# Last block of a hybrid decoder step: projection tiles, gating groups and norm steps in another order

## The reference, cut to what matters

```python
h = rms_norm(x, g_norm) * (1 + scale) + shift
p = h @ w_in                      # h_A, B_A, C_A, z_A, u_B, v_B, z_B
# group A: short gated convolution
s = c_a * h_a
conv = conv_w[0]*s_pad[:, 0:t] + conv_w[1]*s_pad[:, 1:t+1] + conv_w[2]*s_pad[:, 2:t+2]
y_a = b_a * conv * silu(z_a)
# group B: spatial gating in chunks of 128 positions
v_n = layer_norm(v_b, g_v, b_v)
y_b = u_b * (tril(W_s) v_n + b_s) * silu(z_b)
y = concat([y_a, y_b]) @ w_out
out = rms_norm(x + gate * y, g_final)
```

## Time and profile before

| | us |
|---|---|
| median of 3 runs | 347.27 (346.55 to 347.93) |
| the profiled execution | 346.61 |
| its span, slowest core (core 2) | 344.8 |
| spans of all 8 cores | 341.0 to 344.8 |
| TensorE busy, core 2 | 292.3 (85%) |
| VectorE busy, core 2 | 187.4 (54%) |
| GpSimd busy, core 2 | 110.6 (32%) |

### The profile page before, as it was taken

How to read it: one execution, slowest core, us unless ns; L and a number is a source line. 1 busy time by engine, 2 the same in 40 slices (tenths; PEclk the granted TensorE clock), 3 DMA queues, 4 the chain that set the end, 5 groups by cost and what they waited for, 6 DMA issues and landing times.

```text
span 344.8 us, 5627 instructions; the slowest of 8 cores (341.0 to 344.8 us)
## 1 busy us (share of the span) xinstructions
PE 292.3 (85%) x1792; PEld 152.1 (44%) x1792; DVE 187.4 (54%) x350; ACT 122.1 (35%) x215; POOL 110.6 (32%) x161
## 2 busy tenths in 40 slices
PE   0328269996999996999999999999999999999940
PEld 0223134443444443444455444445555557776410
DVE  0321025356464641755778846557864567658972
ACT  2511024127353205624436343444615234242320
POOL 7390265123424213412225443112322122222210
PEclk9999859999999998999999999999999999999995
DMA  5999999999999982075113515101260101516223
GB/s 158 213 156 173 162 165 173 164 230 227 176 176 159 151 183 78 29 204 192 64 60 124 197 49 147 61 22 74 90 237 10 32 0 63 183 63 197 86 117 123
DMA packets 14157, 44.51 MB, mean 129 GB/s; under 512 B 1968, under 2 KB 2352, under 8 KB 13104
## 3 DMA queue, kind: packets, MB, share of 16 engines
q0 software_dynamic: 6624, 21.24, 34.9%
q1 hardware_dynamic: 7504, 22.91, 20.4%
HBM read 51.02 MB, written 8.85 MB: 174 GB/s over the span
## 4 chain that ended last, share of the span: by engine, by line
PE 53%; DMA 24%; DVE 8%; issue 5%; POOL 3%; another core or an unknown queue 3%; ACT 1%; DVEq 1%; POOLq 0%; SPq 0%; ACTq 0%
PE pb L477 32%; PE pb L704 12%; DMA win_bf<-win_l 12%; DMA wada<-wada_l 11%; PE pb L592 5%; DVE ob L802 2%; DMA xc<-x_p 2%; PE pb L403 1%; PE pb L656 1%; PE pb L814 1%; POOL xa L314 1%; DVE ob L723 1%; DVE ob L720 1%; DVE ob L721 1%
## 5 line engine op out<-in xcount | busy, mean ns | idle before, releaser
L477 PE MATMUL pb<-hT,win_bf 128*128 128x512 bf16 (+3 forms) x680 | 127.6, 344 | 3.6 <-ACT tmp L550 2.0
L477 PEld LDWEIGHTS pb<-hT,win_bf 128*128 128x128 bf16 x680 | 66.4, 98 | 60.0 <-issue 6.3
L704 PE MATMUL pb<-wout_bf,yT 128*128 128x512 bf16 (+1 forms) x256 | 58.2, 379 | 1.3 <-POOL yT L676 1.2
L477 PE MATMUL pb<-hT,wh 128*128 128x512 bf16 (+3 forms) x280 | 54.8, 357 | 2.8 <-DVE hT L423 2.8
L676 POOL TENSOR_TENSOR yT<-tmp,tmp 128x512 bf16<-128x512 f32 (+3 forms) x20 | 22.0, 1100 | 67.2 <-DVE tmp L666 38.6
L551 POOL TENSOR_TENSOR yT<-tmp,tmp 128x512 bf16<-128x512 f32 (+3 forms) x20 | 23.7, 1186 | 59.5 <-DVE tmp L546 40.7
L733 ACT ACTIVATE junk<-ob 128x1024 bf16<-128x1024 f32 (+1 forms) x16 | 16.9, 1057 | 70.7 <-DVE ob L723 57.4
L477 PEld LDWEIGHTS pb<-hT,wh 128*128 128x128 bf16 x280 | 27.8, 100 | 27.8 <-issue 7.7
L532 DVE SCALAR_TENSOR_TENSOR tmp<-spad,pv,tmp 128x512 f32<-128x512 f32 (+2 forms) x40 | 26.7, 667 | 20.4 <-ACT tmp L525 13.1
L704 PEld LDWEIGHTS pb<-wout_bf,yT 128*128 128x128 bf16 (+1 forms) x256 | 23.9, 98 | 28.9 <-issue 1.9
L592 PE MATMUL pb<-wv_bf,hT 128*128 128x512 bf16 (+1 forms) x136 | 30.3, 379 | 0.0
(11 more groups left out here) (88 smaller groups left out, 263.5 us busy)
## 6 DMA issues: line engine op xcount, KB each, us to landing
y_p<-ob SPq DMA_DIRECT2D x15, 512.0 KB, 2.7
xc<-x_p SPq DMA_DIRECT2D x14, 512.0 KB, 6.8
wada<-wada_l POOLq DMA_DIRECT2D x6, 1024.0 KB, 34.1
xa<-x_p POOLq DMA_DIRECT2D x10, 512.0 KB, 36.3
win_bf<-win_l POOLq DMA_DIRECT2D x17, 256.0 KB, 40.5
xa<-x_p SPq DMA_DIRECT2D x8, 512.0 KB, 5.1
wout_bf<-wout_l POOLq DMA_DIRECT2D x2, 1024.0 KB, 55.6
wh<-winh_l POOLq DMA_DIRECT2D x4, 256.0 KB, 25.9
```

Source lines behind the costliest of these rows:

```text
L477: ii = pe.matmul(bk.t[:, 0:B.N], lhsT=wsl(m, k), rhs=hT[B.h][:, k, 0:B.N], start=(k == 0), stop=(k == 7))
L704: ii = pe.matmul(bk.t[R, :], lhsT=yT[B.y][:, k, ti * 128:ti * 128 + P], rhs=wout_bf[:, n, k, :], start=(k == 0), stop=(k == 7))
```

## The change

In the last block's second loop, the C step of a tile of the block ahead (`C_mm`, `C_s1`) is issued in front of `GB(B, j)` instead of behind it. `mid` of `GB(B, j)` is now `C_sq` of tile j, not of tile j - 1. `C_s2` of tile j - 1 comes before `GB(B, j)`, between `C_mm` and `C_s1` of tile j. `C_s3` of tile j - 1 stays at the end of step j, which is now behind `GB(B, j)`. At j = 0 the due `C_s3` of the sample rows goes ahead of `newconv`. The set of instructions and their sizes are the same.

```diff
--- before.py
+++ after.py
@@ -1043,17 +1043,18 @@
             newconv(B)
         for j in range(4):
             if last:
-                GB(B, j, (lambda j=j: C_sq(PV, j - 1)) if 0 < j <= npv else None)
+                if j < npv:
+                    C_mm(PV, j, 0, 8)
                 if j > 0:
                     C_s2(PV, j - 1)
                 if j < npv:
-                    C_mm(PV, j, 0, 8)
                     C_s1(PV, j, False)
+                GB(B, j, (lambda j=j: C_sq(PV, j)) if j < npv else None)
                 if j == 0:
-                    newconv(B)
                     while cq:
                         C_s3(*cq.pop(0))
-                elif j < 4:
+                    newconv(B)
+                else:
                     C_s3(PV, j - 1)
                 continue
             if not late and not last:
```

## The result

The changed kernel takes 351.75 us (median of 4 runs, 350.58 to 352.24). The kernel before takes 347.22 us beside it (median of 4, 346.55 to 347.93). The ratio is 1.012, with a 95% interval of 1.0087 to 1.0153: the change costs 4.5 us, between 3.0 and 5.3. The forecast was 350.4 us with a range up to 351.3. So the sign and the mechanism were right, and the size was too small: the median lies 0.45 us above the range. Some executions of every kernel show a lower granted clock on the cores of one die and take some 6% or more longer; the medians, ratios and cores read here leave them out.

A forecast was written before the change was run, and what follows sets the result against it. VectorE was taken to set the last block's pace, with L720 of tile 0 deciding the end. An order loss of 1.83 us plus 1.14 to 1.67 for half clock led to 347.27 + 3.1 = 350.4 us, range 348.7 to 351.3.

The forecast's parts named there:

- the cost of the order: Last block, core 2: tile 0 ends at 331.53, so L720 starts at 331.71 against 329.88, 1.83 us later at full clock.
- What goes: VectorE before tile 0's L720: the 1.42 us power wait and 1.20 us of L802 leave the path, gaining at most 0.90.
- The first cost: VectorE at the first residual load: group 0 now stands behind L723, so the wait grows from 1.33 to 2.05 us.
- The second cost: Slice 6 comes last: group 2's L666 on VectorE starts at 325.52, its GpSimd product at 326.14.
- The third cost: GpSimd's group 2 product, slowed beside tile 1's L802, ends at 327.76, not 326.87; tile 0 starts on TensorE at 327.90.
- TensorE's side: Group 3's matmuls end at 324.4; TensorE idles 3.5 us until 327.90, then tile 0's 16 matmuls take 3.63 us.
- The clock: After that idle stretch TensorE most likely runs tile 0's 16 matmuls at half clock, costing 1.14 to 1.67 us more.
- (a): Late slice 6, slowed GpSimd and half clock: core 2 loses 3.0 to 3.5 us, kernel 350.1 to 350.8; chance 0.62.
- Case (e): Half clock over both last tiles, or longer load waits: up to 4.5 us, kernel to 351.8; chance 0.10.
- (b): TensorE's clock stays up before tile 0: loss 1.83 us, kernel 349.1; chance 0.15.
- (c): GpSimd isn't slowed, idle stretch 2.6 us: loss 0.94 to 2.6 us, kernel 348.2 to 349.9; chance 0.10.
- (d): TensorE isn't held by slice 6, group 2's L666 before about 323.0: 0.90 us won, kernel 346.4; chance 0.03.

The follow-up runs named there:

- the experiment on it: Changed kernel with tile 1's scaling (L802) moved from behind group 2 to behind group 3: 347.68 us, ratio 1.0084 to the kernel before.
- the second run: The changed kernel, unedited, measured once more on the second chip: 348.94 us, ratio 1.0123 to the kernel before.

## Why the prediction was wrong in size and right in kind

Two steps failed: the cost of the order, put at 1.83 us, was 2.36, and the slowest core was worked out with the waits and the clock prices of the cores that were slowest before. By its own steps, on core 2. It had L720 at 331.71 us with full clock; it came at 334.07.

- *What goes.* The wait of 1.42 us for the power became 0.41 us, and L802 of tile 2 runs inside TensorE's stretch. Right, and worth nothing, as forecast: tile 0 is what is late.
- *The first cost.* The wait for the load was forecast at 2.05 us and was 2.33. The load landed 0.14 us later than before, and the last L546 was 0.14 us earlier. The mechanism held.
- *The second cost.* Group 2's L666 was forecast at 325.52 and came at 326.08, 0.56 us later. 0.14 of it is the load. 0.11 is the step from L666 to the 64-row L802, 0.50 us and not the 0.39 of its neighbours. 0.30 is a thing I took as free: the swapped `C_s3` and `newconv` at j = 0 "have the same sum". They have not. The four copies of L565 took 0.40 us to the next instruction before, and take 0.70 us now (317.82 to 318.52). The trace shows why: the 64-row L802, now ahead of them, stretches group 0's product on GpSimd to 1.76 us (316.62 to 318.38), and the first copy, started at 317.82, lasts until that product has ended, 0.58 us instead of 0.16. The other three take 0.16 us each. So it is the third cost once more, at a place where I didn't look for it.
- *The third cost.* The product was forecast at 1.62 us and took 1.63. From its end to the first matmul it took 328.59 - 328.33 = 0.26 us, and not 0.14: another 0.12. Together tile 0 starts 0.14 + 0.11 + 0.30 + 0.01 + 0.12 = 0.68 us later than forecast, 328.59 against 327.90.
- *TensorE's side.* Idle from 324.36, forecast 324.4, for 4.23 us instead of 3.5.
- *The clock.* Forecast 1.14 to 1.67 us; it cost 1.67 (5.30 against 3.63), the upper end, on this core.

The sum for core 2 is 1.83 + 0.69 + 1.67 = 4.19 us, where (a) gave 3.0 to 3.5. The first step that failed is therefore the order's own cost: 1.83 us, where 1.83 + 0.30 + 0.11 + 0.12 = 2.36 was right. It is the same 2.37 that the table gives for core 2's landing before (3.67 us from L546 to L723, so a wait of 2.05 after: 19.66 + 1.88 = 21.54, against 19.17).

The second step that failed is the choice of core. The forecast took the two cores that were slowest, with the waits they had, as the cores that would be slowest after. The wait for the load differs between cores and from one execution to the next (core 2 waited 1.33, 2.33 and 0.80 us in three profiles), and after the change it counts in full, where before it counted less 0.45 us. On top of it comes the clock loss, which hit every core that idled over 3.2 us. The slowest of eight is the one with the worst pair. From core 2's L720 before (329.88) to core 3's after (335.50) it is 5.62 us: 0.08 by the earlier part of the program, 2.37 by the order, 4.32 - 3.67 = 0.65 by the later landing, 2.53 by the clock. The clock's term is the largest of these, and was forecast at 1.67 at most, the higher of the two prices in the earlier trace rows. The length of the idle time doesn't explain the 2.53: core 5 idled 4.57 us as well and lost 1.28. What differs is how long the half clock lasted (shown in the last section). Case (e), "longer waits for the loads ... up to 4.5 us", was the one that came, and I gave it 0.10 and cut part of it from the range, although showed 2.28 us before the change already. It should have been the likeliest case: with eight draws, a wait above 2 us was already there on two cores of before.

Of the rivals, (b) holds for single cores and not for the kernel: core 4 kept its clock after 3.16 us and ended 5.8 us ahead of core 3. (c) is ruled out, since the product was slowed on every core of both runs of the changed kernel, and the experiment on it gave the price. (d) did not occur; group 2's L666 was 3 us later than it needed.

What stays open is what else, beside the idle time, decides whether the clock falls. Another open point is why the load takes 4 to 8 us from issue to landing (issued early it took 7 to 9.3 us, which nothing waited for). It is also open why the half clock lasted longer on two cores, core 3 here and core 1 in the second run, than on all others.

## What to carry to other kernels

Before moving work ahead of a wait on a transfer, ask which instructions run in front of that wait today: they are a cushion, and each one moved behind it makes every late landing cost more. Where the metric is the slowest of several cores, take a wait that differs between cores at its worst and not at its present value on the slowest core. Put each idle stretch that a new order makes in front of a burst of matmuls down with its clock loss, and first try the cheap cure, here loads issued 19 us ahead: with them the changed order costs 1.0 us over before instead of some 4.4, and the old order gains 0.7 us.

## What the runs showed of the hardware

**The clock does not follow the idle time alone.** These are tile 0's 16 matmuls on the eight cores of four runs, 32 in all: the changed kernel twice, the one with early loads, and the one with tile 1 closed late:

| idle before tile 0 | stretches | followed by half clock |
|---|---|---|
| 1.2 to 2.2 us | 15 | 1 |
| 2.3 to 3.2 us | 8 | 4 |
| over 3.2 us | 9 | 9 |

Half clock came after 2.08 us on one core, and full clock stayed after 3.16 us on another. The price was 1.7 us in most cases (5.30 against 3.61 us), 1.28 us once (core 5 of the changed kernel, idle 4.57 us), and 2.5 and 2.75 us on two cores that had idled 4.57 and 4.31 us. So equal idle times had prices of 1.28 and 2.53 us. Core 5 in two stretches, to be laid beside the four of core 3 above:

```profile
328.00:330.00 2.00, 1.84 (x5) 0.73 (x6) 1.59 (x2) 0.00 (x0) 1.10 (x2) 0.50 0.65 262
330.00:332.00 2.00, 2.00 (x9) 0.78 (x7) 0.19 (x1) 0.00 (x0) 0.00 (x0) 0.81 0.46 184
```

Read in slices of 0.2 us, the clock fell at 327.4 us on core 5 and came back at 330.8, and on core 3 it fell at 327.5 and came back at 334.3. Tile 0 began at 328.16 and 329.18. Of its time at half clock, 2.6 and 5.1 us, half is the loss: 1.3 and 2.6 us, against 1.28 and 2.53 measured. On core 1 the clock fell only at 328.1, when the matmuls had been running for 1.2 us. So what a half clock costs is read from how much of it lies over matmuls, not from the idle time ahead.

**GpSimd and VectorE hold each other up, and the one that starts second pays.** A 128x256 product on GpSimd took 0.72 us alone. Begun 0.22 us after a 128-row L802 it took 1.63 us, and begun 0.12 us after the 64-row one 1.76 us, on every core of the changed kernel. Both times it ended some 0.6 us after that L802 (328.33 against 327.76 us, 318.38 against 317.78), while the L802 kept its 1.28 us. The other way round, core 2's product of group 3 began 0.14 us before an L802 and kept its 0.72 us, and that L802 took 1.67 us:

```profile
328.81 0.72 POOL L676 TENSOR_TENSOR yT<-tmp,tmp 128x256 bf16<-128x256 f32 x1
```

From 285 us on the ten profiles hold 168 cases of the first kind, all with a product of 1.57 to 1.64 us beside an L802 of about 1.28, and 32 of the second, all with a product of 0.72 or 0.73 and an L802 of 1.67 or 1.68. The Trainium skill (GPSIMD Engine Reference, section Key points) names this contention for instructions of VectorE with two SBUF inputs; the trace agrees, and adds that only the second to start was slowed.

**Small copies on VectorE pay too.** Four copies of 128x2 elements in the kernel before and in the changed one, core 2 (count, shortest, median and longest in ns), and a like copy in the kernel before:

```profile
L565 DVE COPY ncp_sb<-spad x4: 160/161/162, 315.5 to 315.7; 128x2 f32<-128x2 f32 x4
...
L565 DVE COPY ncp_sb<-spad x4: 155/156/579, 317.8 to 318.5; 128x2 f32<-128x2 f32 x4
...
307.61 0.63 DVE L510 COPY spad<-spad 128x2 f32<-128x2 f32 x1
```

The long one of each kind started while a GpSimd product ran and ended with it: at 318.40 us, where the product ended at 318.38, and at 308.24, where it ended at 308.21. The first is the same on all eight cores of the changed kernel (0.58 us). So such a copy takes 0.16 us or what is left of the product, and a product stretched by an L802 is passed on to the copies behind that L802. No experiment takes this apart from the rest; it is read from the traces.
